# State-space stage in blocks of four tokens, with tables made in the first feed-forward stage, on one Trainium2 core

## The reference

```python
lam_bar = jnp.exp(lam * dt)                       # 64 pairs of groups, 128 states a pair, complex
b_bar = ((lam_bar - 1.0) / lam)[..., None] * (b_re + 1j * b_im)
# for t in 0..255:   state = lam_bar * state + b_bar @ u[t]
#                    y[t]  = real(c_mat @ state) + d_skip * u[t]
z = jax.nn.gelu(y)
out = z * jax.nn.sigmoid(z @ w_glu + b_glu)
```

## Time and profile before

| | before |
|---|---|
| median of three runs | 4101.12 us |
| the profiled execution | 4105.02 us |
| its span, first to last instruction | 4103.7 us |
| PE busy | 3800.0 us, 93% |
| DVE busy | 2565.8 us, 63% |
| ACT busy | 1822.4 us, 44% |
| POOL busy | 1533.1 us, 37% |

### The profile page before, as it was taken

The page is one execution under the profiler, slowest core; times in us unless marked ns, Lnnn a source line. Parts: engine busy times, 40 slices in busy tenths (PEclk is TensorE's granted clock), DMA queues, the critical chain, the costliest instruction groups (busy, mean ns, idle before and its releaser), DMA issues.

```text
span 4103.7 us, 63063 instructions
## 1 busy us (share of the span) xinstructions
PE 3800.0 (93%) x26602; PEld 3228.2 (79%) x26602; DVE 2565.8 (63%) x3645; ACT 1822.4 (44%) x2919; POOL 1533.1 (37%) x725
## 2 busy tenths in 40 slices
PE   5898999999999999989999999998359989999998
PEld 3787888777877887888788888887348878888887
DVE  0435643795368897668664454688985966454457
ACT  1435443654355444545533333442654553343334
POOL 0332443143323440014344444444764434444443
PEclk8999999999999999999999999999679999999999
DMA  9653665345533451034454545453015435554543
GB/s 392 267 214 141 262 241 208 150 177 199 222 151 144 166 190 69 22 121 175 159 186 183 193 180 201 178 204 114 1 63 200 173 141 185 185 190 182 198 178 135
DMA packets 53483, 711.79 MB, mean 173 GB/s; under 512 B 5968, under 2 KB 8144, under 8 KB 10832
## 3 DMA queue, kind: packets, MB, share of 16 engines
q1 hardware_dynamic: 47664, 684.15, 44.3%
q0 software_dynamic: 3472, 21.50, 1.4%
q10 hardware_dynamic: 2064, 2.10, 0.1%
HBM read 705.63 MB, written 2.10 MB: 172 GB/s over the span
## 4 chain that ended last, share of the span: by engine, by line
PE 76%; DVE 15%; ACT 5%; DMA 2%; issue 1%; POOL 1%; SPq 0%; DVEq 0%; ACTq 0%; another core or an unknown queue 0%; POOLq 0%
PE ps L366 43%; PE ps L367 22%; DMA ring<-in_ada 2%; DVE pieces L319 2%; PE ps L2226 2%; PE ps L786 2%; ACT pieces L303 2%; DVE opa L567 1%; DVE r L1169 1%; PE ps L1896 1%; DVE scr L3426 1%; DVE scr L3422 1%; DVE scr L3428 1%; PE ps L1040 1%; PE ps L640 1%
## 5 line engine op out<-in xcount | busy, mean ns | idle before, releaser
L366 PE MATMUL ps<-opa,pieces 128*128 128x512 f32 x6192 | 2254.0, 407 | 64.4 <-DVE pieces L319 45.3
L337 POOL TENSOR_TENSOR pieces<-ring,pieces 128x1024 fp32r<-128x1024 f32 x539 | 1350.2, 2505 | 2227.5 <-ACT pieces L303 2227.4
L367 PE MATMUL ps<-opa,pieces 128*128 128x256 f32 x6192 | 1742.6, 281 | 0.0
L303 ACT ACTIVATE pieces<-ring 128x1024 fp32r<-128x1024 f32 (+1 forms) x1110 | 1098.5, 1036 | 851.5 <-PE ps L367 851.0
L366 PEld LDWEIGHTS ps<-opa,pieces 128*128 128x128 f32 x6192 | 1173.4, 189 | 358.7 <-issue 49.3
L367 PEld LDWEIGHTS ps<-opa,pieces 128*128 128x128 f32 x6192 | 1179.7, 191 | 9.0 <-issue 5.3
L366 PE MATMUL ps<-opb,pieces 128*128 128x512 f32 x2560 | 907.5, 396 | 16.5 <-DVE pieces L319 11.7
L319 DVE TENSOR_TENSOR pieces<-ring,pieces 128x1024 fp32r<-128x1024 f32 (+1 forms) x571 | 709.2, 1242 | 273.3 <-ACT pieces L303 270.9
L367 PE MATMUL ps<-opb,pieces 128*128 128x256 f32 x2560 | 725.1, 283 | 0.0
L366 PEld LDWEIGHTS ps<-opb,pieces 128*128 128x128 f32 x2560 | 482.3, 188 | 137.1 <-issue 16.2
L367 PEld LDWEIGHTS ps<-opb,pieces 128*128 128x128 f32 x2560 | 482.8, 189 | 0.1
(11 more groups left out here) (416 smaller groups left out, 3427.8 us busy)
## 6 DMA issues: line engine op xcount, KB each, us to landing
ring<-in_up SPq DMA_DIRECT2D x64, 2048.0 KB, 7.7
ring<-in_down SPq DMA_DIRECT2D x64, 2048.0 KB, 7.7
ring<-in_win SPq DMA_DIRECT2D x56, 2048.0 KB, 7.7
ring<-in_ada SPq DMA_DIRECT2D x48, 2048.0 KB, 12.0
ring<-in_wout SPq DMA_DIRECT2D x24, 2048.0 KB, 7.7
ring<-in_evin SPq DMA_DIRECT2D x18, 2048.0 KB, 7.8
ring<-in_evout SPq DMA_DIRECT2D x8, 2048.0 KB, 7.7
ring<-in_xkv SPq DMA_DIRECT2D x8, 2048.0 KB, 7.7
```

The lines of the kernel that those rows point to most:

```text
L303: a.do.activation(K.parts_of(p)[0][:, s, :], w[:, s, :], ACT.Copy).then_inc(*K.hi.up((p, h)))
L337: g.do.tensor_tensor(lo[:, s, :], w[:, s, :], hi[:, s, :].bitcast(F), ALU.subtract).then_inc(*K.lo2.up(p))
L366: pe.do.matmul(b[:, 0:512], hi[:, k, :], op[:, 512 * k:512 * k + 512], start=i == 0, stop=False)
L367: t = pe.do.matmul(b[:, 0:256], lo[:, k, :], half(op, 0, k), start=False, stop=i == kt - 1)
```

## The change

The state-space stage takes blocks of four tokens: 16 steps of four pairs with 64 block states each, in place of 32 steps of two pairs with 128. An input or output step of TensorE now covers four steps (`pe_s5_in(s)`, `pe_s5_out(s)`, s = 0 to 3), with products of 64 moving columns and four powers of `lam_bar`. VectorE's instructions for one step keep their kind and size; its difference (first half) and POOL's (second half) are issued a step ahead of the scans. POOL also takes over a product of 128x512 for the angles from ACT.

Seven tables (`TABLES`: the powers 0 to 3 of C, 1 to 3 of B) are made inside the feed-forward of layer 0. `dve_s5_beside` puts one piece in a turn of VectorE, between the feed and the taking of a tile: first the small constants in turns 2, 3, 6, 7, 8 and 10 of the first "up" quarter, then six pieces a table, from turn 16 + 8j (table j of 0 to 3) and 28 + 8j (4 to 6). A piece is one 128x1024 product or a 128x512 product and a 128x512 addition. ACT spreads each table into padded blocks, in 56 copies of 128x512 with a scale from a column (`act_s5_pads`), one a turn behind its own `act_part`. POOL stores 28 blocks of 512 KB in HBM and loads them back in `odin`; SP loads those of s = 1 to 3 in the stage. `odin` loses the constants and tables; it has four groups of direct products of 96 columns, and `pe_s5_in(0)` stands before its last tile. The stage loses the six operations of 128x2048 and the transposes at its start.

```diff
             side = None if q + n else pe_totals(K, ("nf", l))
             pe_tile(K, p + n, K.opa, ("nf", l, "h"), (K.dve, ("usum", l, q, n)), side, 6)
+            if l == 0 and q == 0 and n in (8, 12):
+                pe_s5_rows(K, n // 4 - 2)
...
                 act_next(K, l, n - 1)
+            elif n < 16:
+                next(tables, None)
 
 
...
+            next(tables, None)
             dve_normed(K, p + n, h, K.rstd, ("usum", l, q, n)).then_inc(*K.dve.up())
             v.wait_ge(*K.dve.now())
             v.do.scalar_tensor_tensor(out=s, in0=h, scalar=0.0, in1=h, op0=ALU.max, op1=ALU.mult).then_inc(*K.dve.up(("hsq", l, q, n)))
...
             dve_feed(K, ahead(K, p + n))
             if n and q == 3:
                 dve_next(K, l, n - 1)
+            elif q < 3:
+                next(tables, None)
             dve_onto(K, p + n, xb(K, n), ("down", l, q, n))
...
+TABLES = [("c", k) for k in range(4)] + [("b", k) for k in range(1, 4)]
+TURN0 = 16
+
...
+def first_turn(j):
+
+    return TURN0 + 8 * j + 12 * (j >= 4)
...
+def dve_s5_table(K, j):
+
+    v = K.v
+    which, k = TABLES[j]
...
+        v.wait_ge(*K.act.of(("pad", 4 * j - 5)))
+    dst, src = ([r3(t[:, c, :], g) for c in range(2)] for t in (dst, src))
+    T = r3(K.cross5, g // 2)
+    for c in range(2):
+        v.do.tensor_tensor(dst[c], src[c], a, ALU.mult).then_inc(*K.dve.up())
+        yield
+        for h in range(2):
+            s = slice(g // 2 * h, g // 2 * h + g // 2)
+            v.wait_ge(*K.dve.now())
+            v.do.tensor_tensor(T, src[1 - c][:, s], b[:, s], ALU.mult).then_inc(*K.dve.up())
+            v.wait_ge(*K.dve.now())
+            v.do.tensor_tensor(dst[c][:, s], dst[c][:, s], T, ALU.add if c else ALU.subtract).then_inc(*K.dve.up(("table", j)))
+            yield
+
...
+            a.do.activation(o, i, ACT.Copy, scale=K.half5[which == "b"][:, q:q + 1]).then_inc(*K.act.up(("pad", u)))
+            yield
+
...
+def pool_s5_store(K, u):
+
+    g = K.g
+    g.wait_ge(*K.act.of(("pad", u)))
+    g.do.dma_start(stored_at(K, u), K.pad5[u % 2]).then_inc(*K.kept[u % 2].up(("kept", u), 16))
...
+def pool_s5_beside(K):
+
+    g, p = K.g, K.first["up", 0, 0]
+    store = {first_turn(u // 4) + 7 + 2 * (u % 4) + 3: u for u in range(28)}
+    for t in range(2, 128):
+        if t in store:
...
+def pool_odin(K):
+
+    g, p = K.g, K.first["odin"]
+    kept_all(K, g)
+    load_k(K, g, 2)
+    pool_feed(K, p)
+    g.wait_ge(*K.tile.of(p - 1))
+    load_k(K, g, 3)
+    pool_feed(K, p + 3)
+    g.wait_ge(*K.prod.of(("K", 2)))
+    load_k(K, g, 0)
...
+def sp_s5_tables(K):
+
+    sp = K.sp
+    kept_all(K, sp)
+    sp.wait_ge(*K.tile.of(K.first["odin"] + 15))
+    load_b(K, sp, 1)
+    load_c(K, sp, 1)
+    sp.wait_ge(*K.prod.of(("z5", 3)))
...
+
...
+    for n in range(16):
+        side = None if n else pe_totals(K, ("nm", 1))
+        pe_tile(K, K.first["odin"] + n, K.opa, ("nm", 1, "h"), (K.dve, ("us", n)), side, 6)
+        if n in ORDER_K:
+            pe_s5_direct(K, ORDER_K[n])
+        if n == 14:
+            K.pe.wait_ge(*K.act.of(("K", 1)))
+            pe_s5_in(K, 0)
+
...
+    B = K.BT5[s % 2].rearrange("p (c j i) -> p c j i", c=2, j=16)
+    for m in range(4):
+        for c in range(2):
+            for q in range(4):
+                t = pe.do.matmul(b[32 * q:32 * q + 32, 96 * m:96 * m + 96], B[:, c, 4 * m + q, :], C[:, 0:3, 4 * m + q, c, :],
+                                 start=c == 0, stop=c == 1)
+    t.then_inc(*K.prod.up(("K", s)))
...
+    for s in range(5):
+        if 0 < s < 4:
+            pe_s5_in(K, s)
+        if s == 1:
+            K.pe.wait_ge(*K.dve.of(("u", 15)))
+        if s:
+            pe_s5_out(K, s - 1)
...
+    for q in range(4):
+        if s == 1 and q == 1:
+            pe.wait_ge(*K.dve.of(("u", 15)))
...
+    for m in range(4):
+        for c in range(2):
+            for r in range(4):
+                for q in range(4):
+                    q0 = 32 * q
+                    t = pe.do.matmul(bs[q][:, 256 * c + 64 * m:256 * c + 64 * m + 64], B[q0:q0 + 32, 3 - r, m, c, :],
+                                     K.U[q0:q0 + 32, 4 * s + m, 64 * r:64 * r + 64], start=r == 0, stop=r == 3)
+    t.then_inc(*K.prod.up(("z5", 4 * s + 3)))
...
+    pe.wait_ge(*K.gps.of(("p", 4 * s + 3)))
+    C = K.TC[s % 2].rearrange("p (k j c i) -> p k j c i", k=4, j=16, c=2)
+    direct = K.K5.rearrange("p (m k i) -> p m k i", m=16, k=3)
+    for m in range(4):
+        y = K.bank["y5", s, m // 2][:, 256 * (m % 2):256 * (m % 2) + 256]
...
+    for n in range(17):
+        if n < 16:
+            c, b, M = K.cs5[n % 3], K.bank["z5", n][:, 0:512], K.m5[n % 2]
+            v.wait_ge(*K.prod.of(("z5", n // 4 * 4 + 3)))
             v.wait_ge(*K.act.of(("tab", n)))
...
+        if 0 <= m < 16:
+            wv, rt, M = K.wv5[m % 2], K.rt5[m % 3], K.m5[m % 2]
+            v.wait_ge(*K.dve.of(("zz", m)))
+            v.wait_ge(*K.gps.of(("zz", m)))
+            if m >= 2:
+                v.wait_ge(*K.gps.of(("p", m - 2)))
...
+            v.do.tensor_tensor(M[:, 0:256], M[:, 0:256], M[:, 256:512], ALU.subtract).then_inc(*K.dve.up(("zz", n)))
+        if 0 <= m < 16:
+            v.wait_ge(*K.dve.of(("w", m)))
+            if m >= 8:
+                v.wait_ge(*K.prod.of(("y5", m // 4 * 4 - 5)))
+            v.do.tensor_tensor(K.p5[m % 8][:, 0:512], wv, K.cs5[m % 3][:, 0:512], ALU.mult).then_inc(*K.dve.up(("p", m)))
+        if n >= 6 and n % 4 in (2, 3):
```

More of the change, by code:

```diff
@@ L3126, in dve_odin @@
-def dve_odin(K):
-    v, p = K.v, K.first["odin"]
-    consts = dve_s5_consts(K)
-    for n in range(16):
-        dve_feed(K, ahead(K, p + n))
-        if n == 0:
-            dve_rstd(K, ("nm", 1), K.rstd)
-            v.wait_ge(*K.dve.now())
-        dve_normed_by_parity(K, p + n, K.U[:, n, :], K.rstd, ("us", n)).then_inc(*K.dve.up(("u", n)))
-        if n:
-            next(consts, None)
-    drain(consts)
-def act_s5_consts(K):
+TABLES = [("c", k) for k in range(4)] + [("b", k) for k in range(1, 4)]
@@ L3255, in act_s5_turn @@
-def act_s5_turn(K, m):
-    a = K.a
-    if m == 0:
-        a.wait_ge(*K.load["io5"].of("io5"))
-    else:
-        a.wait_ge(*K.gps.of(("angle5", m - 1)))
-    even = in_pairs(K.io5)[:, :, 0]
-    for z in range(4):
-        j = pair5(2 * m + z // 2, z % 2)
-        t = a.do.activation(K.aq[:, P * z:P * z + P], even, ACT.Copy, scale=K.w5[5][:, j:j + 1])
-    t.then_inc(*K.act.up(("turn", m)))
+    v.wait_ge(*K.prod.of(("row5", 0, 1)))
+    tt(rows_of(K.wide5), over(lim), side, ALU.mult, ("wide5", 1))
@@ new lines, in pe_s5_rows, with act_s5_beside @@
+def pe_s5_rows(K, c):
+    pe = K.pe
+    pe.wait_ge(*K.dve.of(("wide5", c)))
+    pe.wait_ge(*K.dve.of("fold5"))
+    for h in range(2):
+        b, was = K.xb.take(K.act, ("row5", c, h))
+        K.bank["row5", c, h] = b
+        pe.wait_ge(*was)
+        for m in range(8 * h, 8 * h + 8):
+            t = pe.do.matmul(b[:, 64 * (m - 8 * h):64 * (m - 8 * h) + 64], K.wide5[:, P * m:P * m + P], K.fold5, start=True, stop=True)
+        t.then_inc(*K.prod.up(("row5", c, h)))
+def act_s5_beside(K):
+    yield from beside(act_s5_columns(K), *(delayed(first_turn(j) + 7, act_s5_pads(K, j)) for j in range(7)))
@@ new lines, in dve_s5_beside, with delayed, beside @@
+def dve_s5_beside(K):
+    yield from beside(dve_s5_columns(K), *(delayed(first_turn(j), dve_s5_table(K, j)) for j in range(7)))
+def delayed(turns, steps):
+    for _ in range(turns):
+        yield
+    yield from steps
+def beside(*steps):
+    left = list(steps)
+    while left:
+        for g in list(left):
+            if next(g, left) is left:
+                left.remove(g)
+        yield
+def pool_s5_store(K, u):
+    g = K.g
+    g.wait_ge(*K.act.of(("pad", u)))
+    g.do.dma_start(stored_at(K, u), K.pad5[u % 2]).then_inc(*K.kept[u % 2].up(("kept", u), 16))
@@ new lines, in act_odin @@
+def act_odin(K):
+    a, p = K.a, K.first["odin"]
+    for n in range(16):
+        act_feed(K, ahead(K, p + n))
+        if n == 0:
+            act_std(K, ("nm", 1), 1e-5, K.rstd)
+        if n in (0, 2, 6, 8):
+            s = {0: 2, 2: 3, 6: 0, 8: 1}[n]
+            a.wait_ge(*K.load["bt%d" % (s % 2)].of(("bt", s)))
+            a.do.activation(K.BT5[s % 2][:, 512:1024], K.BT5[s % 2][:, 512:1024], ACT.Copy, scale=-1.0).then_inc(*K.act.up(("bt", s)))
+        if n - 1 in ORDER_K:
+            s = ORDER_K[n - 1]
+            a.wait_ge(*K.prod.of(("K", s)))
+            a.do.activation(K.K5[:, 384 * s:384 * s + 384], K.bank["K", s][:, 0:384], ACT.Copy).then_inc(*K.act.up(("K", s)))
@@ L3441, in pool_s5 @@
 def pool_s5(K):
     g = K.g
[L3443 to L3449 removed]
+    p = K.first["odin"] + 13
+    g.wait_ge(*K.hi.of((p, 1)))
+    g.wait_ge(*K.lo.of(p))
+    for rt in K.rt5:
+        g.do.memset(r3(rt, 4)[:, :, 0:1], 0.0).then_inc(*K.gps.up("zeros"))
@@ L3450, in pool_s5 @@
+    for n in range(16):
+        if n % 2 and (n + 3) // 2 < 8:
             pool_s5_angle(K, (n + 3) // 2)
+        if n == 0:
```

(3 more changed lines are left out.)

548 lines of the change are left out of this document (279 added, 269 removed).

## The result

The changed kernel takes 4125.54 us (median of five, 4120.89 to 4131.87) beside 4101.65 of the kernel before in the same five rounds: 1.005 times as long, 95% interval 1.0032 to 1.0068. That is 23.9 us by the medians. Its profiled execution spans 4121.0 us in place of 4103.7, so 17.3 more; what follows finds the place of these 17.3, and the remaining 6.6 lie between executions, where no trace reaches.

What follows compares the result with a forecast made beforehand. It took a full four-engine loop in feed-forward up turns, and VectorE in the state-space stage, as the bounds. Feed-forward +95, `odin` −12 and stage −80 gave +3 us, 4104, range 4070 to 4140.

Steps and rivals of the forecast that it cites:

- Table pieces: Feed-forward, VectorE: 24 pieces in up turns wait for POOL's subtraction, 2.0 us each, 48 in all; those in down turns free.
- Rival B: Feed-forward up turns: the piece starts before POOL's subtraction, costing 1.2 us a turn, 19 us less, 4085; chance 0.18.
- Rival C: Feed-forward: VectorE's idle time takes the pieces, up turns cost near 10 us in all, 4011 to 4030; chance 0.10.
- The reading of the earlier trace: In `odin`, POOL and VectorE ran together and slower: 4.25 us in place of 2.45, 3.42 in place of 1.23.
- Pads: Feed-forward, ACT: 29 padding copies in up turns, ahead of the feed POOL waits for, 0.6 us each, 17.4 in all.
- First quarter: Feed-forward, first quarter: constants, ACT's functions and copies, TensorE's row products and clock add 32 us together.
- `odin`, 104: `odin` without the 128x2048 operations, with direct products and first input group, takes 104 us, a gain of 12.
- Four pauses for instructions: `odin`, TensorE: the 1.98 us wait for "issue" may come four times, adding up to 6 us.
- Stage, 113.7: State-space stage: VectorE's steps and the input and output groups sum to 113.7 us, a gain of 80.
- the chain out(s), in(s+2), p: Stage: output group 15.5 us, input group after next 6.3, then VectorE's turned-back step 5.2, passed twice.
- Rival A: Input groups: loading 32x128 weights sets the rate, 12.8 us in place of 6.3, +19.5, 4123; chance 0.25 with other slower cases.
- Rival D: Stage: POOL or the 2 MB table loads set the time, steps of 6 us, 13 us more, 4117; chance 0.07.

Runs made afterwards that it cites:

- x2: Changed kernel with each table product or addition in up turns replaced by a one-operand sum over fours of the same number of elements; 4078.48 us.
- x1: Changed kernel with all 42 table pieces and 25 of 28 pad pairs moved into down turns, two pieces in four of them; 4070.1 us.
- x3: Changed kernel with VectorE's scan and turning back of steps 3, 7 and 11 issued ahead of the next step's first operation; 4111.47 us.
- x5: Changed kernel with input products taking 32 of the 128 weight columns, moving columns still 64; 4117.22 us.
- x4: Changed kernel with input products taking 32 of their 64 moving columns; 4123.19 us.
- x7_best: Changed kernel with one table piece and one pad pair a down turn, early scans of steps 3, 7, 11, and table loads reordered; 4055.44 us.

## Why the prediction came out as it did

The forecast was +3 us, 4104. The median is 4125.54: inside the range, but above the 4089 to 4113 that had the largest chance. The spans differ by 17.3. By its steps:

- **Table pieces, 2.0 us each: right in place, cause and size.** The turns with a piece and a pad took 8.2 to 8.4 us, 5.65 + 2.0 + 0.6, as written. Quarters 1 and 2 cost 62.6 us by the turns' sum; 48 + 17.4 − 2.6 was 62.8. x2 and the stage's rows beside it show the cause: with one SBUF operand the wait isn't there. Rival B had the other order, the piece first; in the rows POOL was first, by 0.1 us. Rival C (idle time takes them) is refuted in up turns by the 8.3 us and confirmed in down turns by x1. The Trainium skill, "SBUF — State Buffer", section "SBUF: two separate sides", names just this class of VectorE operation, two SBUF inputs against a GpSimd operation that reads SBUF, as an exclusive lock; the trace and x2 agree.
- **The reading of the earlier trace rows was wrong.** I took 4.25 and 3.42 us there as "both ran together and slower". They are the same exclusive wait: L337 starts at 2811.98, L3158 ends at 2813.98, and L337 ends 2.25 us after that, at 2816.23; L319 ends 1.08 us after L337. It had no part in the sum.
- **Pads, 0.6: 0.6 to 0.7 measured** (turns with only a pad 6.3 us).
- **First quarter, 32: 27.7**, within the ± 10 of the forecast. Its parts missed both ways: the trace has two products of 128x2048 at 4.5 us each, behind POOL, where one at 2.3 was counted, and two stops of ACT for other functions at 1.28 each where the forecast had four at 0.9, a figure for which it had no row. That they came out so near is luck.
- **`odin`, 104: 103.4.** The input group took 7.37, not 6.3, and the tiles 5.55 apart, not 5.62. Four pauses for instructions of up to 6 us in all did not come: 1.0 us of "issue" stood ahead of L3426.
- **Stage, 113.7: 130.5** (136.8 less the 6.32 to the first product of `glu`). This is the step that failed, by 16.8. From out(0) on the chain out(s), in(s+2), p is the one that the trace shows, x3 removes its last link for what it costs, and only the sizes were off. Ahead of out(0) a link was missing: the forecast took four steps of VectorE, 24.1, and let p3 wait for nothing, though the code puts it behind in(1) just as p7 behind in(2). The trace has 27.0: 7.4 for in(1)'s table, 13.9 for its 256 products at half clock (1.2 GHz) behind that idle, 5.7 until p3. Where p3 doesn't wait for in(1), POOL's half ends last, and out(0) comes at 25.4 (x3) and 25.9 (x5). So of the 2.9 the missing link is 1.1 to 1.6, and the rest is that the four steps are longer than written. The other terms: in(2) and in(3) took 11.8 and 9.7, not 6.3, +8.9. Output groups 16.7 to 17.7, not 15.5, +4.7 over three. p was quicker, 4.9 for 5.2, −0.5, and the last round 20.8 for 20.1, +0.7.
- **Rival A named what was mis-sized, but its price didn't come.** It kept the 50 ns of 128 moving columns at 64. They fell to 30, near the 25 of the forecast's halving and below the 40 from which I let A decide. Columns count between 128 and 64 and no more between 64 and 32 (x4), and what is left is set by the weight columns (x5). What neither I nor A had was the pace of instructions: 2.71 us of pauses in in(2), 1.69 in in(3), some 3 in each output group. In the earlier trace rows the same wait stood, 1.98 us, and I had priced it only for `odin`.
- **Rival D: a load did stand in the chain,** in(1)'s, for the 1.1 to 1.6 us above. The steps of 6 us that it forecast did not come: the last four took 20.8, 5.2 each.
- **Not in the sum at all:** the 2.9 us behind `glu`. The change gives the result another token order; I counted the instructions that read it as unchanged, since their number and shape are.

Sum: the stage 16.8 and `glu` 2.9 too much, `odin` and the feed-forward 5.4 less than written, make the 14.3 that separate +17.3 from +3. The range held because the terms that were too small came to less than its width, and some of the others paid back 5.4.

## What to carry to other kernels

An engine's idle share says nothing until one turn is followed once round all engines: VectorE was 43% idle, and yet a piece of 1.1 us cost 2.0 in up turns and, one a turn, at most 0.9 us for a whole quarter of down turns, where it has 3.3 us to spare (x7_best). Put side work where the lead is longer than the piece plus POOL's instruction that it will wait for, and one piece there, not two. When a step is replaced by many short products, price four things apart: the moving columns, the weights' time, the pace at which instructions arrive, and the clock after an idle. And follow every engine's order from the first group on: here the missing link stood ahead of the first round, before the pattern repeats.

## What the runs showed of the hardware

- A VectorE instruction with two SBUF operands waits for a running POOL subtraction to end (2.86 us for 0.69); one with a single SBUF operand does not, neither a reduction (0.70) nor a product of 128x512 whose other operand is in PSUM (0.67).
- Products of 64 moving columns: 30 ns with weights of 32x128, 15.5 with 32x32, at full clock. With weights of 32x128, 128 moving columns took 50 ns and 32 the same as 64.
- In in(3) 128 short products take at least 4.16 us, at 30 ns each as at 15.5, with pauses of 0.3 to 4.5 us in in(2) and in(3) that the profile calls "issue", and a load beside them more or less changed nothing that could be measured. In `odin` 256 took 7.37 us without a pause.
- TensorE after an idle of 7.4 us ran 256 products at a granted clock of 0.50, 54 ns each in place of 29; after one of 2.16 us it ran the next 3 us at 0.50.
- ACT's copy of 128x256 took 0.31 us when read in storage order and 0.55 in steps of 64 elements.
